# Up projection's tokens moved to an array of their own: rows of 260 columns, every panel's rows at one place modulo 256 bytes

## What is computed

```
xn  = rmsnorm(h) @ w_in            # 3 token mixers and 3 gates
mix = sum_i sigmoid(gate_i) * (branch_i @ w_i_o)
h   = h + mix @ w_o
u   = causal_dwconv3(rmsnorm(h) @ w_up)      # w_up: 2048 x 11264
h   = h + (silu(u_gate) * u_up) @ w_down     # w_down: 5632 x 2048
out = rmsnorm(h)[16:]
```

## Time and profile before

| | |
|---|---|
| median of 3 runs | 1746.93 us (1746.3 to 1746.97) |
| span of the profiled execution, first to last instruction | 1745.1 us |
| around the span (median less span) | 1.8 us |
| TensorE busy (matmul) | 1734.3 us, 99% |
| VectorE busy | 1117.8 us, 64% |
| ScalarE busy | 763.7 us, 44% |
| UP's stretch of the span | 990.2 to 1492.8 us |

### The profile page before, as it was taken

How to read it: one execution, slowest core, us unless ns; L and a number is a source line. 1 busy time by engine, 2 the same in 40 slices (tenths; PEclk the granted TensorE clock), 3 DMA queues, 4 the chain that set the end, 5 groups by cost and what they waited for, 6 DMA issues and landing times.

```text
span 1745.1 us, 34098 instructions
## 1 busy us (share of the span) xinstructions
PE 1734.3 (99%) x13429; PEld 1680.7 (96%) x13429; DVE 1117.8 (64%) x1607; ACT 763.7 (44%) x921; POOL 263.3 (15%) x494
## 2 busy tenths in 40 slices
PE   9999999999999999999999999999999999999998
PEld 8999999999999999999999999999999999888886
DVE  6857766667565554555556687777777777554454
ACT  6635444354354444444444444334444444343433
POOL 3153332630530000000000043321000000000000
PEclk9999999999999999999999999999999999999999
DMA  8567557666565655556645566666555565665654
GB/s 232 169 180 186 168 149 198 176 175 178 153 184 181 189 178 178 175 182 194 201 159 192 181 195 192 204 200 192 183 182 181 180 186 180 223 190 189 189 192 134
DMA packets 310296, 320.62 MB, mean 184 GB/s; under 512 B 17353, under 2 KB 285133, under 8 KB 310093
## 3 DMA queue, kind: packets, MB, share of 16 engines
q1 hardware_dynamic: 296861, 311.01, 58.2%
q0 software_dynamic: 12928, 7.80, 2.0%
q10 hardware_dynamic: 432, 0.79, 0.1%
HBM read 311.10 MB, written 2.11 MB: 179 GB/s over the span
## 4 chain that ended last, share of the span: by engine, by line
PE 99%; DVE 0%; DMA 0%; ACT 0%; SPq 0%; issue 0%; ACTq 0%; DVEq 0%
PE ps L1435 27%; PE ps L1437 27%; PE ps L1436 27%; PE ps L1693 5%; PE ps L1692 5%; PE ps L1691 5%; PE ps L1526 0%; DMA xb<-in_x_dram 0%; PE ps L1540 0%; PE ps L1565 0%; PE ps L1555 0%; PE ps L1556 0%; PE ps L1584 0%; PE ps L1585 0%; DVE xl L941 0%; DVE lo L896 0%
## 5 line engine op out<-in xcount | busy, mean ns | idle before, releaser
L896 DVE TENSOR_TENSOR lo<-raw,hi 128x1024 fp32r<-128x1024 f32 x584 | 709.9, 1229 | 494.4 <-ACT hi L627 490.2
L1435 PE MATMUL ps<-xh,hi 128*128 128x260 f32 (+1 forms) x3328 | 945.8, 284 | 0.2 <-DVE xl L941 0.2
L1437 PE MATMUL ps<-xh,lo 128*128 128x260 f32 (+1 forms) x3328 | 941.7, 283 | 0.0
L1436 PE MATMUL ps<-xl,hi 128*128 128x260 f32 (+1 forms) x3328 | 936.5, 281 | 0.0
L627 ACT CAST hi<-raw 128x1024 fp32r<-128x1024 f32 x584 | 604.8, 1048 | 671.8 <-PE ps L1437 539.0
L1436 PEld LDWEIGHTS ps<-xl,hi 128*128 128x128 f32 x3328 | 626.6, 188 | 0.2
L1435 PEld LDWEIGHTS ps<-xh,hi 128*128 128x128 f32 x3328 | 625.2, 188 | 1.3 <-issue 0.4
L1437 PEld LDWEIGHTS ps<-xh,lo 128*128 128x128 f32 x3328 | 624.7, 188 | 0.0
L610 POOL DMA_DIRECT2D hT<-h2b x128 | 69.6, 553 | 604.3 <-DVE h2b L1289 599.7
L1693 PE MATMUL ps<-lo,act_h 128*128 128x512 f32 x350 | 138.5, 396 | 0.0
L1692 PE MATMUL ps<-hi,act_l 128*128 128x512 f32 x350 | 137.3, 392 | 0.0
(11 more groups left out here) (298 smaller groups left out, 1383.6 us busy)
## 6 DMA issues: line engine op xcount, KB each, us to landing
raw<-in_w_in_dram SPq DMA_DIRECT2D x224, 512.0 KB, 3.6
raw<-in_w_up_dram SPq DMA_DIRECT2D x176, 512.0 KB, 4.6
raw<-in_w_down_dram SPq DMA_DIRECT2D x88, 512.0 KB, 4.7
raw<-in_w_o_dram SPq DMA_DIRECT2D x32, 512.0 KB, 3.4
raw<-in_w_in_dram SPq DMA_DIRECT2D x32, 256.0 KB, 4.2
raw<-in_w_a_o_dram SPq DMA_DIRECT2D x16, 512.0 KB, 4.3
raw<-in_w_b_o_dram SPq DMA_DIRECT2D x16, 512.0 KB, 3.3
raw<-in_w_c_o_dram SPq DMA_DIRECT2D x16, 512.0 KB, 3.3
```

The lines of the kernel that those rows point to most:

```text
L896: nc.vector.tensor_tensor(part(ph, i, q, lo_all), raw[:, s, :], part(ph, i, q, hi_all).bitcast(F32), ALU.subtract).then_inc(lo_ready, 1)
L1435: nc.tensor.matmul(acc, w_hi, mh, start=first and j == 0, stop=False)
L1436: nc.tensor.matmul(acc, w_hi, ml, start=False, stop=False)
L1437: ins = nc.tensor.matmul(acc, w_lo, mh, start=False, stop=last and j == KJ - 1)
```

## The change

UP's tokens leave `xh` and `xl` and get an array `xu` of 8704 columns in their place (the same 34,816 bytes; `act_h`, `act_l` and everything behind keep their addresses). `UP_H` and `UP_L` say at which column of `xu` the 260-column row of each of the 16 `kt` starts. `xu` starts at place 32. With it the rows of `kt` 0 to 3, which panels 0 and 4 of a trip move, all stand at place 0; those of `kt` 4 to 7 at 240; of 8 to 11 at 32; of 12 to 15 at 176, high and low alike.

```
--- before.py
+++ after.py
+        xn_scope.close()
+        UP_H = (824, 1912, 3000, 4088, 564, 1652, 2740, 3828, 0, 1088, 2176, 3264, 292, 1380, 2468, 3556)
+        UP_L = (5176, 6264, 7352, 8440, 4916, 6004, 7092, 8180, 4352, 5440, 6528, 7616, 4644, 5732, 6820, 7908)
+        xu = sb("xu", [P, 8704], F32R, upx)
...
+        def up_high(kt):
+            return xu[:, UP_H[kt]:UP_H[kt] + NC]
+        def up_low(kt):
+            return xu[:, UP_L[kt]:UP_L[kt] + NC]
...
 ScalarE, WO:
-            with act.Fori(0, WO.trips) as i:
+            for i in range(WO.trips):
...
-                            ins = nc.scalar.activation(xh[:, bass.ds(i * 4 + (2 * pair + n), 1), Q0:T]...,
-                                                       hT[...], ACT.Copy, scale=par[...])
+                            kt = i * 4 + 2 * pair + n
+                            ins = nc.scalar.activation(up_high(kt)[:, QW:], hT[:, kt, Q0:T], ACT.Copy, scale=par[:, N2 + kt:N2 + kt + 1])
...
 VectorE, WO:
-            with dve.Fori(0, WO.trips) as i:
+            for i in range(WO.trips):
...
+                            kt = i * 4 + 2 * pair + n
+                            for row in (up_high(kt), up_low(kt)):
+                                nc.vector.memset(row[:, 0:QW].bitcast(F32), 0.0)
                             ins = nc.vector.scalar_tensor_tensor(
-                                out=xl[:, one, Q0:T], in0=hT[:, one, Q0:T], scalar=par[...],
-                                in1=xh[:, one, Q0:T].bitcast(F32), op0=ALU.mult, op1=ALU.subtract)
+                                out=up_low(kt)[:, QW:], in0=hT[:, kt, Q0:T], scalar=par[:, N2 + kt:N2 + kt + 1],
+                                in1=up_high(kt)[:, QW:].bitcast(F32), op0=ALU.mult, op1=ALU.subtract)
...
 TensorE:
+            def up_window(kt0):
+                return lambda j: (up_high(kt0 + j), up_low(kt0 + j))
...
-                    use_panel(UP, i, q, st, x_window(kq * KJ, C0, NC), NC, kq == 0, kq == 3)
+                    use_panel(UP, i, q, st, up_window(kq * KJ), NC, kq == 0, kq == 3)
```

More of the change, by code:

```diff
@@ L295, in hybrid_layer @@
         br_out.close()
+        xn_scope.close()
+        UP_H = (824, 1912, 3000, 4088, 564, 1652, 2740, 3828, 0, 1088, 2176, 3264, 292, 1380, 2468, 3556)
+        UP_L = (5176, 6264, 7352, 8440, 4916, 6004, 7092, 8180, 4352, 5440, 6528, 7616, 4644, 5732, 6820, 7908)
+        upx = ExitStack()
+        xu = sb("xu", [P, 8704], F32R, upx)
         upt = ExitStack()
@@ L303, in hybrid_layer @@
         upt.close()
-        xn_scope.close()
+        upx.close()
         NG = D // DCOLS
@@ L798, in _ @@
                         for n in range(2):
-                            ins = nc.scalar.activation(xh[:, bass.ds(i * 4 + (2 * pair + n), 1), Q0:T].rearrange("p a t -> p (a t)"),
-                                                       hT[:, bass.ds(i * 4 + (2 * pair + n), 1), Q0:T].rearrange("p a t -> p (a t)"),
-                                                       ACT.Copy, scale=par[:, bass.ds(i * 4 + (N2 + 2 * pair + n), 1)])
+                            kt = i * 4 + 2 * pair + n
+                            ins = nc.scalar.activation(up_high(kt)[:, QW:], hT[:, kt, Q0:T], ACT.Copy, scale=par[:, N2 + kt:N2 + kt + 1])
                         ins.then_inc(h2_hi, 1)
@@ L1272, in _ @@
                         for n in range(2):
-                            one = bass.ds(i * 4 + (2 * pair + n), 1)
+                            kt = i * 4 + 2 * pair + n
+                            for row in (up_high(kt), up_low(kt)):
+                                nc.vector.memset(row[:, 0:QW].bitcast(F32), 0.0)
                             ins = nc.vector.scalar_tensor_tensor(
-                                out=xl[:, one, Q0:T], in0=hT[:, one, Q0:T], scalar=par[:, bass.ds(i * 4 + (N2 + 2 * pair + n), 1)],
-                                in1=xh[:, one, Q0:T].bitcast(F32), op0=ALU.mult, op1=ALU.subtract)
+                                out=up_low(kt)[:, QW:], in0=hT[:, kt, Q0:T], scalar=par[:, N2 + kt:N2 + kt + 1],
+                                in1=up_high(kt)[:, QW:].bitcast(F32), op0=ALU.mult, op1=ALU.subtract)
                         ins.then_inc(h2_lo, 1)
```

## The result

The changed kernel takes 1753.75 us (median of 5 runs, 1753.24 to 1754.89) against 1746.93 us before in the same session (5 runs, 1746.3 to 1747.09). The ratio is 1.0040, with a 95% interval of 1.0029 to 1.0051: 0.4% slower, 6.8 us. The forecast was 1741.8 us, and the range ended at 1751.0.

What follows compares the result with a forecast made beforehand. TensorE's matmul pace was taken to bound the kernel. UP's places gave -5.1 us, memsets and loops nothing: span 1745.1 to 1740.0 us, plus 1.8 us for the median, 1741.8 us; range 1735.5 to 1751 us.

Steps and rivals of the forecast that it cites:

- What bounds the kernel: Whole kernel: TensorE, busy 1734.3 of 1745.1 us at full clock; columns streamed and their pace set the end.
- memsets, written-out loops and VectorE's share: WO and UP: 32 memsets and the unrolled WO loop cost nothing; VectorE's share in UP goes from 76% to 77%.
- the price of the places: UP's matmuls: rows held at the new places take 117.7 ns instead of 118.9, saving 1.2 ns each.
- three panels of four should gain and one not: UP's panels: those at 0, 240 and 32 run at 117 ns a matmul, the one at 176 at 120.
- The term, -5.1 us: UP: 1.2 ns saved on each of 4224 matmuls, 5.1 us in all.
- DN's percent: DN's start: 512-column rows at places 128 and 112 differ by 0.9 to 1.0%; taken over to UP as 1.2 ns.
- The cost of standing still: UP, in the slower rival: a bad place, met by one matmul in four, is afterwards met 24 times in a row.
- The slower rival: UP: held rows collide with the weight tile, place 0 costing 2.0 ns, others 1.1; 5.6 us more, 1752.5 us; chance 0.23.
- No change: Rival, UP: four other places average the same as the old; 1745.6 us, anything from 1743.4 to 1750.4; chance 0.27.
- The 117.3 ns for 256 columns: End of DN: 12 matmuls at place 112 start 117.3 ns apart, 10.6 over their columns, no better than UP's 10.5.
- Much faster: Rival, UP: excess comes mostly from changing place; alike rows shed 3.5 ns a matmul, 14.8 us, 1732.1 us; chance 0.08.
- The cachelines of the Trainium skill: UP's rows: 1040 bytes cover 65 16-byte lines before and after, so by that rule zero gain, 1746.9 us.

Runs made afterwards that it cites:

- experiment 1: Changed kernel with its rows put back at the old places 80, 144, 208, 16 inside every panel; array, memsets and written-out loop kept: 1746.86 us, ratio 1.000.
- experiments 2 and 3: Against the changed kernel: first the old places, one held per panel, 1748.04 us; then the new places walked in turn within each panel, 1746.62 us.
- experiments 3 and 4: Against the changed kernel: new places walked within each panel, 1746.62 us; then eight other places, one held per panel, in two kernels, 1749.91 and 1750.89 us.
- experiment 3: Changed kernel with the four new places walked: each panel's rows stand at 0, 240, 32 and 176 in turn; 1746.62 us, ratio 1.000.
- e6: Changed kernel with the weight tiles of all phases 16 bytes lower, at place 112 instead of 128; UP's rows unmoved: 1754.15 us.
- e8: Changed kernel with the old places walked, UP's rows moved with 258 columns instead of 260, memsets gone: 1751.36 us, ratio 1.0028.
- e15: Changed kernel with the old places walked, UP's rows moved with 256 columns, leaving out the last two tokens, memsets gone: 1745.98 us.
- e1: Changed kernel with the old places 80, 144, 208, 16 walked inside every panel: 1746.86 us, 2.853 us a panel.
- e3: Changed kernel with the new places 0, 240, 32, 176 walked inside every panel: 1746.62 us, 2.853 us a panel.
- e12: Changed kernel with the weight tiles of all phases 64 bytes lower, at place 64, in DN too; UP's rows unmoved: 1755.71 us.

## Why the prediction was wrong

- **What bounds the kernel** was right. TensorE's pace in UP decided everything; memsets, written-out loops and VectorE's share cost nothing (experiment 1), and the median stood as far over the span as forecast (1.8 us before, 1.75 after).
- **The step that failed** is the price of the places, "three panels of four should gain and one not", 117.7 ns a matmul. Measured: 121.1 (0), 121.7 (240), 120.2 (32) and 119.2 (176), mean 120.5; the one panel expected to lose lost least. The term, -5.1 us, measured +7.0. Three things were wrong in it. First, the times of single rows within a walked panel were taken as times of places held, and experiments 2 and 3 show that these are not the same. 16 is indeed the quickest alike, but 208, which I read as slow, is the second quickest. It was not slow in the walk either: read to 1 ns, the triples of that panel take 352, 360, 355, 353 and 361, 358, 359, 355 ns, and the printed starts, rounded to 10 ns, hid it. Second, the neighbour was taken to be like its neighbour: 0 and 32 lie 16 bytes from 16 and take 68 and 46 ns a panel more. Third, DN's percent showed that 16 bytes can matter, by 0.9%, and I used it as a sign, too; from place 16 to place 0 they cost 2.4%.
- **The cost of standing still** was seen in the rival only. The two walks at 2.853 are quicker than 12 of the 16 places held, and 23 ns quicker than the mean of all 16, which makes 4.1 us of the 7 (experiments 3 and 4).
- **The slower rival** had the sign, and its core right, that a bad place is met by 24 matmuls in a row. That its size came close (1752.5 against 1753.75) is luck: it was added up from a price for each place, and experiment 3, where the same places are met as often but in turn, shows that these prices are not paid there. Its particulars were wrong, too: a multiple of 128 is not the bad distance, since 0 is slow and 128, the tile's own place, is the third quickest.
- **No change** was argued from an average over places. For the two walks it comes out exactly (2.853 for both sets), but the change did not walk, and other orders of the old places took up to 2.873. The 117.3 ns for 256 columns in its support is 118.0 when the starts are read to 1 ns, 11.3 over the columns and not 10.6.
- **Much faster** is refuted: alike rows shed 0.6 ns a matmul at best.
- **The cachelines of the Trainium skill** ("SBUF — State Buffer", "Door 1: The DMA port swizzle") gave no change, since the lines crossed are 65 either way. The runs do not agree: 65 lines took 2.839 to 2.920 us a panel here, and 258 and 260 columns, both 65 lines, took 2.880 and 2.853.

What stays open is why. The runs show that the place of the weight tile counts together with that of the moving row, that with all tiles moved by 64 bytes the times go by the distance to 11 ns while with 16 bytes they miss it by up to 38, and that a panel inherits from the one ahead. Traffic of the other engines is not the cause, as far as the traces tell: from the second trip on each panel's time repeats from trip to trip to 1 ns in both kernels, and before the change it is 2.853 us in WO as in UP, with VectorE busy for 62% and 76%. The traces do not show which part of the memory or of the engine makes a matmul wait, and no rule here gives the table.

## What to carry to other kernels

Where TensorE is the bound and the clock is full, the addresses of its operands can matter: here a panel with its rows at one place took from 0.5% less to 2.3% more than the walk. No smooth reading of a trace predicted this: measure each candidate, with the rest of the panel's order as it will be. Holding one place for a whole panel was slower at 12 of 16 places. A walk is no safe default either. Two walks ran at 2.853 us, but the old places in other orders took 2.865 and 2.873, and the old order itself took 2.867 behind another panel and in WO with the tiles 16 bytes lower. When the total moves by less than it can tell, the distance between first matmuls of neighbouring panels still tells it to 1 ns.

## What the runs showed of the hardware

- The pace of fp32r matmuls of 260 columns depends on the place of the weight tile, too: moving all tiles by 16 bytes took WO from 118.9 to 119.5 ns a matmul with its rows unmoved (e6). The Trainium skill, "TensorE: Matmul & The Clock Gate", "Step-by-step: what each phase is for", says that loading the next tile's weights does not steal read bandwidth from the running matmul. A pace that moves with the tile's place does not agree well with that for fp32r, though no run here shows what a matmul waits for.
- 258 columns ran slower than 260 (120.0 against 118.9 ns, e8), and 256 hardly faster (118.6, e15).
- Two quite different walks over four places give the same 2.853 us a panel, to the nanosecond (e1, e3).
- With one place and one tile distance for 24 matmuls in a row, the steps between their starts still differ: 115 to 129 ns at place 240 in the changed kernel.
- 512-column rows take 233.3 ns at places 64 and 128 and 231.1 at 112, with stationary tiles at 32 (e12 and the changed kernel).
